# Decoder step on one core: V and Z of a head pair computed in that pair's own attention phase, unit halves in fixed PSUM banks, two out blocks taken jointly, and another way to spread row maxima

## The reference

```python
def chunk_mlp_mixer(h, ...):
    p = h @ w_in + b_in                      # width 3 * 2048
    u, v, z = gelu(p_u), gelu(p_v), p_z
    sg = spatial_gate(layer_norm(v))
    return (u * sg * silu(z)) @ w_out + b_out    # 2048 -> 1024: the "out blocks"

x = layer_norm(alpha * x + (1 + gate) * mixer(h))
k, v, logf = x @ kv_w + kv_b                 # 1024 each, log_sigmoid on 16 columns
q, z = split(h @ w_in + b_in)                # h = x * (1 + scale) + shift
logits = q k^T / 8 + c_q - c_k               # c: running sums of logf, causal
o = softmax(logits) @ v
y = (o * silu(z)) @ w_out + b_out            # then DeepNorm and layer norm again
```

## Time and profile before

| | us |
|---|---|
| median of three runs | 1831.62 (1830.38 to 1832.17) |
| profiled execution | 1832.32 |
| its span | 1830.7 |
| busy: TensorE / VectorE / ScalarE / GpSimd | 1683.2 / 996.8 / 623.6 / 426.5 |
| mean granted clock of TensorE | 0.955 |

### The profile page before, as it was taken

One profiled execution on the slowest core, in us unless ns is written; L12 is line 12 of the kernel. 1 busy time (PEld: TensorE's weight loads), 2 busy tenths in 40 slices (PEclk: granted clock), 3 DMA queues, 4 the chain that ended last, 5 costly groups with the idle time before them and its releaser, 6 DMA issues.

```text
span 1830.7 us, 28121 instructions
## 1 busy us (share of the span) xinstructions
PE 1683.2 (92%) x10192; PEld 1463.2 (80%) x10192; DVE 996.8 (54%) x1552; ACT 623.6 (34%) x980; POOL 426.5 (23%) x432
## 2 busy tenths in 40 slices
PE   6999999999999979999679999999999999759985
PEld 4899999999999969999567778787777778447742
DVE  3423353434343463245534676766767776789775
ACT  2311221111111153235322546463644546252121
POOL 0000011101110100002210526253443526354221
PEclk9999999999999999999889999999999999669987
DMA  8111121222122203234222221212112120418757
GB/s 348 35 46 46 34 91 60 92 82 80 67 92 80 82 23 116 92 119 146 69 73 70 81 59 58 85 48 85 46 69 69 57 79 35 141 36 274 247 231 299
DMA packets 50191, 180.45 MB, mean 99 GB/s; under 512 B 6522, under 2 KB 8186, under 8 KB 48850
## 3 DMA queue, kind: packets, MB, share of 16 engines
q1 hardware_dynamic: 31650, 116.11, 18.7%
q0 software_dynamic: 18480, 63.53, 9.7%
HBM read 154.07 MB, written 17.15 MB: 94 GB/s over the span
## 4 chain that ended last, share of the span: by engine, by line
PE 76%; DVE 10%; issue 4%; ACT 4%; POOL 2%; DMA 2%; POOLq 0%; DVEq 0%; SPq 0%; ACTq 0%
PE bank L1669 20%; PE bank L1671 18%; PE bank L1670 18%; PE bank L1944 2%; PE bank L1993 2%; PE bank L1801 2%; POOL p_lo L524 2%; PE bank L1975 2%; PE bank L1974 2%; PE bank L1995 2%; PE bank L1994 2%; DVE pages L1364 1%; DMA fsw<-units 1%; PE bank L1781 1%; DVE scol L1367 1%
## 5 line engine op out<-in xcount | busy, mean ns | idle before, releaser
L1669 PE MATMUL bank<-h_hi,w_lo 128*128 128x344 f32 x1152 | 373.8, 325 | 8.1 <-DVE h_lo L1052 8.0
L1670 PE MATMUL bank<-h_lo,w_hi 128*128 128x344 f32 x1152 | 367.9, 319 | 0.0
L1671 PE MATMUL bank<-h_hi,w_hi 128*128 128x344 f32 x1152 | 367.7, 319 | 0.0
L524 POOL TENSOR_TENSOR p_lo<-parg,p_hi 128x512 fp32r<-128x512 f32 (+1 forms) x192 | 220.6, 1165 | 178.9 <-ACT p_hi L899 177.7
L1669 PE MATMUL bank<-x_hi,w_lo 128*128 128x512 f32 x528 | 223.8, 424 | 11.3 <-POOL x_lo L481 6.4
L1669 PEld LDWEIGHTS bank<-h_hi,w_lo 128*128 128x128 f32 x1152 | 217.0, 188 | 13.4 <-issue 9.2
L1670 PEld LDWEIGHTS bank<-h_lo,w_hi 128*128 128x128 f32 x1152 | 217.1, 188 | 0.2 <-issue 0.2
L1671 PEld LDWEIGHTS bank<-h_hi,w_hi 128*128 128x128 f32 x1152 | 216.8, 188 | 0.0
L1670 PE MATMUL bank<-x_lo,w_hi 128*128 128x512 f32 x528 | 211.4, 400 | 0.0
L1671 PE MATMUL bank<-x_hi,w_hi 128*128 128x512 f32 x528 | 211.4, 400 | 0.0
L1669 PE MATMUL bank<-y_hi,w_lo 128*128 128x320 f32 (+2 forms) x512 | 179.5, 351 | 25.7 <-ACT y_hi L720 9.4
(11 more groups left out here) (298 smaller groups left out, 2680.2 us busy)
## 6 DMA issues: line engine op xcount, KB each, us to landing
raw<-units SPq DMA_DIRECT2D x121, 512.0 KB, 3.4
ada_ring<-w_ada SPq DMA_DIRECT2D x32, 512.0 KB, 3.3
pages<-cache_k POOLq DMA_DIRECT2D x32, 512.0 KB, 5.5
pages<-cache_v POOLq DMA_DIRECT2D x32, 512.0 KB, 7.4
ada_first<-w_ada SPq DMA_DIRECT2D x8, 1024.0 KB, 14.9
ckb<-scr_c POOLq DMA_DIRECT2D x16, 512.0 KB, 4.4
KX<-KA SPq DMA_DIRECT2D x32, 256.0 KB, 4.2
xT<-x_t SPq DMA_DIRECT2D x2, 2064.0 KB, 23.3
```

The costliest lines, as they stand in the source:

```text
L524: g.tensor_tensor(p_lo[:, r, off:HALF], parg[:, r, off:HALF], p_hi[:, r, off:HALF].bitcast(F32), ALU.subtract).then_inc(S("p_ready"), 1)
L1669: mm(out, lhs_lo, rhs_hi, start=first, stop=False)
L1670: mm(out, lhs_hi, rhs_lo, start=False, stop=False)
L1671: return mm(out, lhs_hi, rhs_hi, start=False, stop=last)
```

## The change

The units of a pair now come in the order K, Q, V, Z, so the scaled ones are Q and Z. The prelude has only K and Q of pair 0. Phase `j` has V and Z of pair `j` (32 steps) and then K and Q of pair `j + 1` (32 steps); the last phase has 32 steps where it had none. Half 0 of every unit is in bank 0 and half 1 in bank 1; the sample rows go to bank 1, ahead of step 3 (2 for Q, V and Z) rather than step 0.

The transposes of V stand after step 20 of its own phase and use banks 6 and 7; `v_lo` comes before the last `peak`. `z_evac` is split in two, with other work between: the first instruction takes the bank, and `z_gate` forms the product later, for which `zth` has two halves. `spread` is two matmuls of 512 columns for each half instead of eight of 128; their moving operand `md` (the identity times the maxima) is made by VectorE in two instructions of 128 x 512, where a copy of 128 x 8 stood. The out blocks 0 and 1 are done jointly, block 1 three `k` behind block 0, and the units of both are split in the course of the `y` split. In the last phase the scores 3 to 5 go behind `y2_low`, to the start of the out-projection; the samples' query (`turn(1, 0)`, `tok(1, ...)`) moves to the middle of the phase, and the eight page loads stand between GpSimd's products instead of ahead of them.

```diff
-        KIND = (0, 2, 1, 3)
-        FOLD_AT = (5, 3, 2, 2)
+        KIND = (0, 1, 2, 3)
+        SCALED = (1, 3)
+        ROWS_AT = (3, 2, 2, 2)
+        FOLD_AT = (6, 5, 5, 4)
+        SPLIT_AT = {1: U_OUT + 1, 9: U_OUT + 2, 12: U_OUT + 3}
...
# TensorE
+            def joint_step(bb, k):
+                if k % KB == 0:
+                    pe.wait_ge(S("lo_ready"), U_OUT + 2 * (k // KB) + bb + 1)
+                if bb == 0:
+                    pe.wait_ge(S("y_split"), k // 2 + 1)
+                    wait(pe, S("y_split_odd"), (k + 1) // 2)
+                last = out_step(bb, k, bb)
+            for s in range(2):
+                for k in range(s * KB, (s + 1) * KB):
+                    joint_step(0, k)
+                    if k - LAG >= s * KB:
+                        joint_step(1, k - LAG)
+                for k in range((s + 1) * KB - LAG, (s + 1) * KB):
+                    joint_step(1, k)
...
-                    last = sample_rows(bank(q % 2)[:, 0:P], slot, hS if q >= 2 else x1S)
+                if n == ROWS_AT[q]:
+                    wait(pe, *((S("zs_done"), 4 * j - 1) if q == 0 else (S("ev_h"), 6 * j + 2 * q)))
+                    last = sample_rows(bank(1)[:, 0:P], slot, hS if q in SCALED else x1S)
...
-                last = token_step(bank((q + half + 1) % 2), slot, half, k)
+                last = token_step(bank(half), slot, half, k)
...
             def spread(j, half):
-                    for t in range(4):
-                        i = 4 * half + t
-                        last = mm(ps[1][:, h, t * P:(t + 1) * P], nminr[:, h, i:i + 1].broadcast_to([P, P]), identr[:, :], ...)
+                    pe.wait_ge(S("nr_ready"), 4 * j + 2 * half + h + 1)
+                    last = mm(ps[1][:, h, :], ones[:, :], md[:, h, :], start=True, stop=True)
...
-            for q in range(4):
+            for q in range(2):
                 for n in range(16):
...
                 def steps(a, b):
                     for n in range(a, b):
-                        if more:
-                            step(j + 1, n // 16, n % 16)
+                        m = 2 + n // 16
+                        if more or m < 4:
+                            step(j + m // 4, m % 4, n % 16)
...
# VectorE, order in the prelude (split_lo(0, 1) stands ahead of take_samples(0, 0)) and in a phase
             take_samples(0, 1)
+            split_lo(0, 2)
             evac_s(0, 1)
-            split_lo(0, 2)
-            take_samples(0, 2)
...
                 exponents(j, 0)
+                z_evac(j, 0)
                 exponents(j, 1)
+                z_gate(j, 0)
+                split_lo(j + 1, 0)
+                exponents(j, 2)
+                z_evac(j, 1)
...
-            for n in range(6, EARLY):
+            for n in range(3, EARLY):
                 score(n)
...
# GpSimd, last phase
-            load_set(cache_k, 0, 0)
+            load_page(cache_k, 0, 0, 0)
+            p_low(KB - 1, 3)
+            load_page(cache_k, 0, 0, 1)
+            load_page(cache_k, 0, 0, 2)
+            p_low(KB - 1, 4)
```

More of the change, by code:

```diff
@@ L366, in _ @@
                 for s in range(2):
-                    if bb != 1 or s != 0:
+                    if bb != 1:
                         load(U_OUT + 2 * bb + s, s)
                 if bb == 0:
-                    load(U_OUT + 2, 0)
+                    for u in range(U_OUT + 2, U_BOTH):
+                        load(u, u % 2)
                     sp.wait_ge(S("y_lo_ready"), WB)
@@ L556, in _ @@
                 phase(j)
+            scale(KB - 1, 3, 0, KB)
+            store_v(KB - 1)
+            for c in range(3):
+                p_low(KB - 1, c)
             pool.wait_ge(S("ev_s"), 4 * KB)
@@ L1386, in peak_round @@
                 dve.wait_ge(S("nl_ready"), 16 * j + 8 * half + 8)
-                v.tensor_copy(nminr[:, :, 4 * half:4 * half + 4], nmin[:, :, 4 * half:4 * half + 4])\
-                    .then_inc(S("nr_ready"), 1)
+                if half == 1:
+                    dve.wait_ge(S("b_done"), 2 * j + 1)
+                for h in range(2):
+                    v.tensor_tensor(md[:, h, :].rearrange("p (t q) -> p t q", t=4), over(ident[:, :], 4),
+                                    wide(nmin[:, h, 4 * half:4 * half + 4], P), ALU.mult).then_inc(S("nr_ready"), 1)
             def key_decay(j):
@@ L1726, in _ @@
             for h in range(2):
-                last = mm(ps[3][:, h, :], ones[:, :], wsT[:, 4 * h:4 * h + 4, :], start=True, stop=True)
+                last = mm(ps[3][:, h, :], ones[:, :].bitcast(F32), wsT[:, 4 * h:4 * h + 4, :], start=True, stop=True)
             last.then_inc(S("rs_mm"), 1)
@@ L1766, in sample_sums @@
                     pe.wait_ge(S("s_sum"), 2 * n - 1 + i)
[L1767 removed]
+                    mm(bank(SUMS[n])[:, 0:NS], ones[:, :].bitcast(F32), red[:, :], start=True, stop=True).then_inc(S("s_mm"), 1)
             def turn_ada(out, n):
@@ L1833, in ln_backward, with out_step @@
                 last.then_inc(S("ln1_back"), 1)
+            def out_step(bb, k, slot):
+                for out, c0, c1 in out_parts(bb):
+                    last = three(out, w_hi[:, slot, k % KB, :], w_lo[:, slot, k % KB, :], y_hi[:, k, c0:c1], y_lo[:, k, c0:c1],
+                                 k == 0, k == WB - 1)
+                return last
             def unit_out(bb, s):
@@ L2026, in phase @@
                 peak(j, 1)
-                if not more:
-                    pe.wait_ge(S("ev_s"), 4 * KB)
-                    pe.wait_ge(S("zs_done"), 4 * KB)
-                    turn(1, 0)
                 steps(6, 9)
@@ L2056, in phase @@
                 values(j, 2)
+                if not more:
+                    pe.wait_ge(S("zs_done"), 4 * KB)
+                    turn(1, 0)
                 steps(37, 38)
```

295 lines of the change are left out of this document (132 added, 163 removed).

## The result

| | before | after |
|---|---|---|
| median, same session (8 runs each) | 1831.4 (1829.66 to 1832.72) | 1836.6 (1833.99 to 1840.04) |
| profiled execution / its span | 1832.3 / 1830.7 | 1834.0 / 1832.5 |

What follows compares the result with a forecast made beforehand. It took a phase to be bound by its TensorE matmuls and the out-projection to be close to VectorE's bound. Terms -10.2 - 21.5 + 0.7 - 3.0 + 9 = -25.0 gave 1807 us, range 1793 to 1823.

Steps and rivals of the forecast that it cites:

- Steady phases: Seven attention phases: savings and new VectorE delays nearly cancel, +0.1 us per phase, +0.7 in all, bounds -5 to +7.
- a `w_lo` beside GpSimd's products took 2.31 us, and step 32 needs it: +0.9: Steady phases: the gate's second instruction (0.69) and K's w_lo stand between exponents, costing 0.9 us per phase.
- a saving of 0.45: Steady phases: two wide spread matmuls save 0.95 us per phase, and the late md gives back 0.5.
- The first rival: From last peak to step 32, VectorE's chain sets each phase; 1841 us at 5 us each; slower case, chance 0.06.
- Last phase: Phase that gains 32 projection steps: 78.8 us instead of 81.9, -3.0 us, between -9 and +4.
- Out blocks: Blocks 0 and 1 done jointly during the y split: waits filled, end at 700.9, gain 10.2 us, 7 to 12.
- the lower end: Out blocks: gain of only 7 us if a weight load comes late by three more.
- Prelude: Before phase 0: two units leave, TensorE idles 12.9 us before the fold; -19.4 and -2.1, together -21.5, between -16 and -27.
- phase 0 starts near 965: Sign that the forecast is right: phase 0 starts at 965.3 instead of 984.70 after the shorter prelude.
- Start of the out-projection: Three more scores on VectorE ahead of the next block's w_lo; TensorE idles about 6 us; +9, between +5 and +10.

Runs made afterwards that it cites:

- experiment 1: Kernel after with K's w_lo moved from behind the second exponents and Z's gate to ahead of the seventh peak: 1805.7 us, ratio 0.9866.
- experiment 4: Kernel after with the spread as before (eight small matmuls, no md) and K's split left late: 1831.4 us, ratio 1.0004.
- experiment 5: Kernel after with the spread as before and K's w_lo moved early, ahead of the seventh peak: 1801.4 us, ratio 0.9854.
- experiment 6: Kernel before with only the joint out blocks 0 and 1 added: 1823.2 us, ratio 0.9969.
- experiment 9: Kernel after with the w_lo of the out-projection's second unit ahead of the five scores: 1835.6 us, ratio 1.0033.
- experiment 10: Kernel after with K's w_lo moved early and scores 3 to 5 back in the last phase: 1800.2 us, ratio 0.9856.
- experiments 3 and 2: 3: kernel after, GpSimd's low-part products cut for two chunks in phases 1 to 6, 1812.6 us. 2: kernel after, Z's gate behind K's w_lo, 1816.0 us.
- experiment 8: Kernel after with the first unit's sample rows and bias ahead of the second unit's w_lo in the prelude: 1828.9 us, ratio 0.9994.
- experiment 11: Kernel after with K's w_lo early, sample rows first in the prelude, and score 3 in the last phase: 1792.8 us, ratio 0.9813.

## Why the prediction was wrong

- **Steady phases (+0.7, measured +24.7).** This is the step that failed, in the sentence "a `w_lo` beside GpSimd's products took 2.31 us, and step 32 needs it: +0.9". I had the place, the cause and nearly the length of `w_lo` (2.01), and mis-sized what follows from them. Only `w_lo` was priced beside GpSimd; the gate ahead of it was put in at its lone 0.69 us and the mask not at all, while they took 1.50 and 1.57. The wait was counted without the clock: 2.21 us of idle time cost 3.9 (experiment 1), 1.6 of them by the clock (experiment 4). And the spread was counted as a saving of 0.45, while it costs 0.65 a phase (experiment 5). From +0.1 to +3.7.
- **The first rival** was this mechanism, at its place, with "It decides from 25/7 = 3.6 us per phase"; it got 0.06. The evidence against it was VectorE's 24 free microseconds in a phase. That is a sum over the phase: between the last maxima and this `w_lo` VectorE idled for about half a microsecond.
- **Last phase (-3.0, measured +0.9).** The same step again: K's late split stands in the last phase too and costs 3.9 us there. Without it (experiment 1) the phase is 78.6 us long for my 78.8. That this fits so well is partly luck: score 0's product of 3.71 us (4.12 in experiment 1), and the 4.42 us for which TensorE idles behind it in both, were not in my sum. In the kernel after:

```profile
1619.10 3.71 DVE L1384 TENSOR_TENSOR pages<-pages,qb 128x1024 f32<-128x1024 f32 x1 [0.69 <-DMA qb<-scr_q]
```

- **Out blocks (-10.2; -8.1 in the profiled execution, 5.7 in the ratio of experiment 6).** Mechanism right. In the profiled execution block 2 starts at 702.65 for my 700.9, and the lower clock behind the change of units, which I had not counted there, cost 1.6 us. In nine of eleven traces the load is late as well, and block 2 waits up to 3 us, as it is issued only at 695; I had named that as the lower end.
- **Prelude (-21.5, measured -23.3).** Right: `samp` behind the scaled `w_lo`, 11.92 us of gap for my 12.9. Two slips in the working don't touch this: the terms from 942.6 on add up to 964.7 and not 965.3, and "phase 0 starts near 965" left out the gain of the out blocks ahead of it. It started at about 957.
- **Start of the out-projection (+9, measured +7.5).** Right, and so was its reason: with the order changed the wait only moved (experiment 9), with three scores fewer it went (experiment 10).

## What to carry to other kernels

Where a wait in a loop is priced, follow the queue of the engine that ends it instruction by instruction, each at its length beside what runs then, and look at the granted clock behind the wait. If an instruction's inputs are ready long before its turn, its place in the queue is free to choose: here an idle stretch some 16 us ahead was worth 3.9 us a phase, more than the engine time that the change saved. Free time summed over a phase says nothing of a place in it.

## What the hardware showed

- The same wait of 2.2 us left the granted clock at 1.00 once and brought it to 0.50 in other phases of the same execution (experiment 4); in the kernel after, phase 0 was spared (2.31 us, clock 1.00) and the other phases not. Behind the waits of 0.65 and 0.80 us of experiments 3 and 2 the mean clock of all steady phases was 1.00. But a wait of 0.99 us between the out blocks, behind one of 0.51, brought it to 0.58 in the kernel after, and left it at 1.00 in experiment 8 with the same two waits.
- A VectorE product of two SBUF operands that takes 1.22 us alone took 3.71 and 4.12 us beside GpSimd, and 1.23 in experiment 11, where GpSimd's two products took 3.07 us for 2.52; a sum with one input kept its 1.22.
- One 512 KB load, issued at the same place of the program, landed 4.2 to 6.1 us after its issue in eleven executions.
